# A two-layer transformer block: compressed scores in fp32r halves, later column splits on GpSimd, and one gathered u row per plain expert column

## The reference

```python
kc = compress(k_cmp, cmp_k_w1, cmp_k_w2)                      # 31 compressed keys
s_c = jnp.einsum('bqgrd,bngd->bgrqn', qblk, kc) * scale
p_c = masked_softmax(s_c, cmp_end[None, :] <= t[:, None])
...
mixed = jnp.concatenate([rmsnorm_2(o_a, out_gain_a), rmsnorm_2(o_b, out_gain_b)], axis=-1) @ w_out
h = x + mixed
...
vals, ci = lax.top_k(cand, P_TOPK)                            # 16 picks e, gates g per head
a = jnp.einsum('cd,ckd->ck', xc, expert_u[ec])
w = (gc * jax.nn.gelu(a.astype(jnp.float32))).astype(x.dtype)
y = jnp.einsum('ck,ckd->cd', w, expert_v[ec])
```

## Time and profile before

| what | value |
|---|---|
| device time, 3 runs | median 2398.34 us (2397.9 to 2403.95) |
| the profiled execution | 2400.16 us |
| its span | 2398.3 us |
| mean granted PE clock | 0.998 of full speed |
| busy: PE, DVE, ACT, POOL | 2370.4 (99%), 1706.7 (71%), 822.8 (34%), 1088.0 (45%) us |
| attention | about 967 to 1119 us from the span's start |
| plain u columns, spread, last plain u columns | 1279 to 1553, 1553 to 1801, 1801 to 1868 us |
| v columns | 1875 to 2394 us |

### The profile page before, as it was taken

The page is one execution under the profiler, slowest core; times in us unless marked ns, Lnnn a source line. Parts: engine busy times, 40 slices in busy tenths (PEclk is TensorE's granted clock), DMA queues, the critical chain, the costliest instruction groups (busy, mean ns, idle before and its releaser), DMA issues.

```text
span 2398.3 us, 35569 instructions
## 1 busy us (share of the span) xinstructions
PE 2370.4 (99%) x12528; PEld 2056.0 (86%) x12528; DVE 1706.7 (71%) x2818; ACT 822.8 (34%) x1401; POOL 1088.0 (45%) x711
## 2 busy tenths in 40 slices
PE   8999999999999999999999999999999999999999
PEld 6888888878888887888889999999999888888887
DVE  8888885463433656784718699798886788888887
ACT  4132222100112314675325333344443333333333
POOL 6777766666666550100654888721112322222220
PEclk9999999999999999999999999999999999999999
DMA  4333324333332222200224899999999999999995
GB/s 150 97 105 105 105 86 136 132 109 110 133 119 96 88 81 87 74 4 7 72 95 134 293 311 306 308 350 347 343 332 409 376 361 348 356 355 355 347 361 197
DMA packets 181336, 490.46 MB, mean 205 GB/s; under 512 B 14848, under 2 KB 80512, under 8 KB 181248
## 3 DMA queue, kind: packets, MB, share of 16 engines
q1 hardware_dynamic: 144384, 355.12, 43.5%
q0 software_dynamic: 36864, 134.23, 15.0%
HBM read 436.86 MB, written 52.43 MB: 204 GB/s over the span
## 4 chain that ended last, share of the span: by engine, by line
PE 91%; POOL 3%; issue 3%; DVE 1%; ACT 1%; DMA 0%; SPq 0%; DVEq 0%; POOLq 0%; ACTq 0%
PE ps L726 40%; PE ps L1327 22%; PE ps L1287 18%; POOL spl L2669 2%; PE ps L1161 2%; PE ps L1308 2%; PE ps L1138 1%; POOL rare L2679 1%; PE ps L1124 1%; PE ps L910 1%; PE ps L1084 1%; PE ps L1030 1%; PE ps L831 0%; PE ps L1128 0%; PE ps L1127 0%
## 5 line engine op out<-in xcount | busy, mean ns | idle before, releaser
L1287 PE MATMUL ps<-hh,spl 128*128 128x384 f32 x2048 | 535.3, 337 | 2.9 <-POOL spl L2669 2.9
L726 PE MATMUL ps<-hh,spl 128*128 128x512 f32 x1728 | 535.3, 389 | 1.5 <-DVE x L1978 0.8
L1327 PE MATMUL ps<-spl,wsp 128*128 128x512 f32 x2304 | 523.8, 389 | 0.0
L1327 PEld LDWEIGHTS ps<-spl,wsp 128*128 128x128 f32 x2304 | 432.1, 188 | 89.2
L1691 ACT ACTIVATE spl<-ring 128x1024 fp32r<-128x1024 f32 x256 | 271.9, 1062 | 679.9 <-PE ps L1327 331.9
L2574 POOL TENSOR_TENSOR spl<-ring,spl 128x1024 fp32r<-128x1024 f32 (+1 forms) x164 | 427.7, 2608 | 13.1
L726 PEld LDWEIGHTS ps<-hh,spl 128*128 128x128 f32 x1728 | 324.4, 188 | 69.5 <-DVE x L1978 1.2
L1287 PEld LDWEIGHTS ps<-hh,spl 128*128 128x128 f32 x2048 | 371.1, 188 | 6.0 <-issue 5.4
L2572 POOL CAST spl<-ring 128x1024 fp32r<-128x1024 f32 (+1 forms) x164 | 185.8, 1133 | 400.6 <-PE ps L726 380.1
L1287 PE MATMUL ps<-hl,spl 128*128 128x384 f32 x1024 | 342.5, 334 | 0.0
L2473 DVE TENSOR_TENSOR spl<-ring,spl 128x1024 fp32r<-128x1024 f32 x192 | 235.2, 1225 | 148.5 <-ACT spl L1691 140.4
(11 more groups left out here) (443 smaller groups left out, 3375.1 us busy)
## 6 DMA issues: line engine op xcount, KB each, us to landing
ring<-stream_in SPq DMA_DIRECT2D x134, 512.0 KB
ring<-u_in SPq DMA_DIRECT2D x128, 512.0 KB
ring<-v_in SPq DMA_DIRECT2D x128, 512.0 KB
ring<-stream_in SPq DMA_DIRECT2D x60, 704.0 KB
gelu<-gst SPq DMA_DIRECT2D x128, 192.0 KB
dense<-stage SPq DMA_DIRECT2D x12, 2048.0 KB
gl<-gelu SPq DMA_DIRECT2D x32, 768.0 KB, 7.1
gw<-dense SPq DMA_DIRECT2D x32, 768.0 KB, 9.6
```

The source lines that it names most:

```text
L726: m = pe.matmul(ps[:, bank, :], w[:, part, k0 + k * n:k0 + k * n + P], rhs(k), start=first and k == 0 and part == 0 and rhs is high, stop= ...
L1287: m = pe.matmul(ps[:, bank, 0:TD], w[:, part, k0 + k * P:k0 + (k + 1) * P], rhs(k), start=first and k == 0 and part == 0 and rhs is high, ...
L1327: m = pe.matmul(ps[:, bank, :], wsp[:, j % 2, part, tok], spl[:, j % 2, row, cols], start=False, stop=last and n == 2)
```

## The change

1. `kcz` becomes 2 groups x 2 parts (high, low) x 32 in fp32r, with a zero in the 32nd place. DVE makes it in three dependent steps (one product, four casts, four subtractions) in place of four products; the compressed scores are eight fp32r matmuls in place of four float32 ones; readers of the scores step over 32 columns in place of 31.
2. The bias of a step is a TENSOR_SCALAR with a per-partition scalar in place of a TENSOR_TENSOR.
3. POOL's four output-projection columns of the attention stretch all come in quarters, behind the second, fifth, eighth and last weighing of a branch, in place of: two whole ones behind `mid_ready`, one behind the third weighing, one behind the last.
4. `A_ROOT` is two steps later and stands ahead of the evacuation of its iteration; `A_TURNS` and `A_INVERSE` are two steps later.
5. `gathers_by(e)` is one per column from 12 to 63, 52 in all; `AMONG_DOTS` is 44 (before 50), `EARLY_DOTS` 52 (before 58). The spread keeps 8 a pass, so 28 dots are left beside the last plain columns (before 22).
6. Tiles behind `kcz` move by 128 elements; nothing else is done with them.

```diff
-AMONG_DOTS, EARLY_DOTS, SPREAD_DOTS = 50, 58, 8
+AMONG_DOTS, EARLY_DOTS, SPREAD_DOTS = 44, 52, 8
...
-PLACED, FIRST_DOTS, LAST_DOTS = 12, 16, 60
+PLACED = 12
...
 def gathers_by(e):
 
-    if e < FIRST_DOTS:
-        return min(2 * (e - PLACED + 1), ROW_SLOTS)
-    return ROW_SLOTS + AMONG_DOTS * min(e - FIRST_DOTS + 1, LAST_DOTS - FIRST_DOTS + 1) // (LAST_DOTS - FIRST_DOTS + 1)
+    return e - PLACED + 1
...
-        kcz = sb("kcz", [P, A_G, N_CMP], c=two)
+        kcz = sb("kcz", [P, A_G, 2, P // TT], F32R, c=two)
...
-        A_SQUARES, A_ROOT = A_H * PER + 6, A_H * PER + 10
-        A_TURNS = [A_H * PER + 13 + 4 * k for k in range(TT)]
+        A_SQUARES, A_ROOT = A_H * PER + 6, A_H * PER + 12
+        A_TURNS = [A_H * PER + 15 + 4 * k for k in range(TT)]
...
-        A_INVERSE = A_H * PER + 14
+        A_INVERSE = A_H * PER + 16
...
                     for t in range(TT):
-                        pe.matmul(bank[:, t * N_CMP:(t + 1) * N_CMP], query(at, g)[:, t * P:(t + 1) * P].bitcast(F32), kcz[:, g, :],
-                                  start=t == 0, stop=False)
+                        for part in range(2):
+                            pe.matmul(bank[:, t * CMP_ROWS:(t + 1) * CMP_ROWS], query(at, g)[:, t * P:(t + 1) * P], kcz[:, g, part, :],
+                                      start=t == 0 and part == 0, stop=False)
...
             for u in range(NS + TURN_LAG):
                 if u < NS:
                     probs(*STEPS[u])
+                if u == A_ROOT:
+                    eng.wait_ge(o_squares, TT)
+                    o_inverse_root(NORM_SUMS[0])
                 if u >= TURN_LAG and not on_dve(u - TURN_LAG):
                     turned(u - TURN_LAG)
                 if A_SQUARES <= u < A_SQUARES + TT:
...
-                elif u == A_ROOT:
-                    eng.wait_ge(o_squares, TT)
-                    o_inverse_root(NORM_SUMS[0])
                 elif u - 1 in A_TURNS:
...
-                    o = dve.tensor_tensor(s_[:, 3:4], s_[:, 0:1], root_of(n, qt), ALU.mult)
+                    o = dve.tensor_scalar(s_[:, 3:4], s_[:, 0:1], root_of(n, qt), None, ALU.mult)
...
-            for g in range(A_G):
-                lo, part = slice(g * A_D, (g + 1) * A_D), slice(g * N_CMP, (g + 1) * N_CMP)
-                for half in halves:
-                    o = dve.tensor_tensor(kcz[half, g, :], kcn[lo, 0, part], ps[lo, 6 + (3 + B_H) % 2, part], ALU.mult)
+            step(dve.tensor_tensor(kcn[:, 0, :], kcn[:, 0, :], ps[:, 6 + (3 + B_H) % 2, 0:A_G * N_CMP], ALU.mult))
+            placed = [(g, half, kcn[g * A_D:(g + 1) * A_D, 0, g * N_CMP:(g + 1) * N_CMP]) for g in range(A_G) for half in halves]
+            for g, half, normed in placed:
+                o = dve.tensor_copy(kcz[half, g, 0, 0:N_CMP], normed)
+            step(o)
+            for g, half, normed in placed:
+                o = dve.tensor_tensor(kcz[half, g, 1, 0:N_CMP], normed, kcz[half, g, 0, 0:N_CMP].bitcast(F32), ALU.subtract)
             o.then_inc(mid_ready, 1)
...
                 if c < 4:
-                    if c < 2:
-                        pool.wait_ge(mid_ready, 1)
-                        unit_parts(u % RING, N_SPLIT + c + 1, w=out_w[c])
-                        continue
-                    pool.wait_ge(at_weighed, 3 if c == 2 else A_DONE)
+                    pool.wait_ge(at_weighed, (2, 5, 8, A_DONE)[c])
```

More of the change, by code:

```diff
@@ L309, in build @@
         kz = sb("kz", [P, 2 * A_G, T], F32R, c=two)
-        kcz = sb("kcz", [P, A_G, N_CMP], c=two)
+        kcz = sb("kcz", [P, A_G, 2, P // TT], F32R, c=two)
+        sb("kcz_end", [P, 62], c=two)
         pre = ExitStack()
@@ L342, in build @@
         w7 = sb("w7", [P, 2, D], F32R, c=two)
-        sb("w7_end", [P, 3, T], c=two)
         a_parts = [(oah[:, k, :], oah[:, 4 + k, :] if k < 2 else il1[:, k - 2, :]) for k in range(4)]
@@ L1117, in scores @@
                     for t in range(TT):
-                        pe.matmul(bank[:, t * N_CMP:(t + 1) * N_CMP], query(at, g)[:, t * P:(t + 1) * P].bitcast(F32), kcz[:, g, :],
-                                  start=t == 0, stop=False)
-                    pe.matmul(bank[:, 0:TT * N_CMP], identb[:, :], cmpb[:, :, :].rearrange("p a n -> p (a n)"),
+                        for part in range(2):
+                            pe.matmul(bank[:, t * CMP_ROWS:(t + 1) * CMP_ROWS], query(at, g)[:, t * P:(t + 1) * P], kcz[:, g, part, :],
+                                      start=t == 0 and part == 0, stop=False)
+                    pe.matmul(bank[:, 0:P].rearrange("p (t n) -> p t n", t=TT)[:, :, 0:N_CMP], identb[:, :], cmpb[:, :, :],
                               start=False, stop=True).then_inc(at_s, 1)
@@ L1615, in probs @@
                         o = eng.activation(pr[:, u // TT % 2, u % TT, t * CMP_ROWS:t * CMP_ROWS + N_CMP],
-                                           ps[:, u % TT, t * N_CMP:(t + 1) * N_CMP], ACT.Exp, bias=bias[:, t:t + 1],
+                                           ps[:, u % TT, t * CMP_ROWS:t * CMP_ROWS + N_CMP], ACT.Exp, bias=bias[:, t:t + 1],
                                            scale=root_of(n, t), accum_out=total[:, t:t + 1])
@@ L2237, in tops @@
                     top = cmp_state(n)[0]
-                    step(dve.tensor_reduce(top, ps[:, u % TT, 0:TT * N_CMP].rearrange("p (t n) -> p t n", t=TT), AX_X, ALU.max,
+                    step(dve.tensor_reduce(top, ps[:, u % TT, 0:P].rearrange("p (t n) -> p t n", t=TT)[:, :, 0:N_CMP], AX_X, ALU.max,
                                            negate=True))
@@ L2259, in early_bias @@
                 biases(*STEPS[u])
+            for g in range(A_G):
+                for part in range(2):
+                    dve.tensor_copy(kcz[:, g, part, N_CMP:], zero[:, :])
             for h in range(4):
@@ L2649, in _ @@
                 if c < 4:
-                    if c < 2:
-                        pool.wait_ge(mid_ready, 1)
-                        unit_parts(u % RING, N_SPLIT + c + 1, w=out_w[c])
-                        continue
-                    pool.wait_ge(at_weighed, 3 if c == 2 else A_DONE)
+                    pool.wait_ge(at_weighed, (2, 5, 8, A_DONE)[c])
                     slot, w = u % RING, out_w[c]
-                    pool.tensor_copy(w[:, 0, :], ring[:, slot, 0:D]).then_inc(wt_high, 1)
+                    pool.tensor_copy(w[:, 0, 0:D], ring[:, slot, 0:D]).then_inc(wt_high, 1)
                     pool.wait_ge(wt_high, N_SPLIT + c + 1)
```

## The result

The changed kernel takes 2410.62 us (median of 8 runs, 2407.55 to 2415.81) against 2400.78 (8 runs, 2397.9 to 2403.95); the ratio is 1.0043, with a 95% interval of 1.0034 to 1.0051. It is slower, by about 10 us. The profiled execution took 2410.3 us, its span is 2408.4, the mean granted PE clock 0.996.

The account below looks back on a forecast made before the run. PE, busy 99% of the span, was taken as the bound. Attention start -1.0, compressed scores 0, root and chunks +3.4, one gather per column +3.1 and six gathers +0.5 gave +6.0 us: 2404.3 us, range 2393 to 2412.

Parts of the forecast that it names:

- the likeliest case: Whole kernel: the summed forecast, 2404.3 us for the median; 2398 to 2409 got chance 0.45.
- D: Last plain columns: six more dots and gathers cost +0.5 us, bounds 0 and +7.5.
- A's new places: Attention: POOL's moved output columns could hold only DVE's small products, with PE's scores four steps ahead: 0.
- B: MLA attention: moving the root and the mixing chunks two steps later costs +3.4 us.
- Start of attention: First compressed scores: POOL's hold and its half clock go, later keys bring a 1.9 us wait and half clock: -1.0 us.
- Compressed scores: Attention heads: eight fp32r passes cost the same as four float32 matmuls' eight passes: 0, bounds +-0.8 us in all.
- Root and chunks: MLA attention: root's wait and clock gain, four 1.4 us waits for ACT and one half clock cost: +3.4 us.
- One gather per column: Plain u columns: 5.3 us gained, but a 7 us wait for the picks' read and half clock: +3.1 us net.
- Six more gathers beside the last plain columns: Last plain u columns: full DMA engines take 3.1 MB more, DVE holds: +0.5 us, bounds 0 and +7.5.
- Rival 3: Last plain columns: six gathers' 7.5 us all return as late ring loads, +7 more, 2411 us; chance 0.12.
- Rival 2: MLA stretch: each of four 1.4 us waits is followed by half clock, 2409.4 us; chance 0.25.
- rival 1: Attention and gathers: chunk turns don't wait, start keeps full clock, gather 51 lands soon: -9 us, 2389; chance 0.12.

Follow-up runs that it names:

- e5: Changed kernel with POOL's first three output columns behind the third, sixth and ninth weighing instead of second, fifth and eighth: 2408.05 us (one run).
- e7: Changed kernel with the compressed keys in plain float32 again, with scores, readers and DVE's making as before the change: 2409.05 us (one run).
- e4: Changed kernel with the mixing chunks and the inverse back at their old places, the root left two steps later: 2406.36 us, ratio 1.0023.
- e2: Changed kernel with its 52 gathers out by column 60, double at columns 12, 13 and 14: 2406.24 us, ratio 1.0017.
- e3: Changed kernel without the transfers of the last six gathers of u rows, their dots kept: 2404.39 us, ratio 1.0012.
- g3: g1 with 55 gathers by column 60, three columns double, 25 left for the last plain columns: 2392.5 us, ratio 0.996.
- g4: g2 with the three early 1.5 MB loads behind ring loads of columns 125, 126, 127 instead of 123, 125, 127: 2396.36 us, ratio 0.9979.
- g1: Changed kernel with float32 keys, POOL's columns behind weighings 3, 6, 9, chunks back, 58 gathers by column 60 from column 9: 2389.64 us, ratio 0.9953.
- g2: g1 with 52 gathers, one per column from 9 to 60, 28 left for the last plain columns: 2394.6 us, ratio 0.9974.

## Why the prediction was right, and where not

The forecast was 2404.3 us within 2393 to 2412, with 0.50 on no difference that can be told and 0.38 on slower. The measured 2410.6 is in the range and on the side that had 0.38: the likeliest case was 6 us short. (By the shares given to the rivals, slower adds up to 0.25 + 0.12 + 0.045 = 0.415.) That it stayed in the range is in part luck, since an error in one term made up for others: D was 7.2 too low and A's new places 1.6, B was 2.5 too high, and the start of attention 0.3. With B as forecast it would have come to about 2413.

- **Start of attention** (-1.0): PE's waits ahead of and behind the first compressed scores and the half clock sum to -1.3 (+1.1, then -2.4). The wait for the keys was given as 1.9 and is 2.06, the one of 1.94 behind it is gone, and half clock followed. Right.
- **"In their new places only DVE's small products could be held ... 0"**: wrong. Three heads grew from 11.2 to 11.73 to 11.75 us, +1.6 in all: the held product stands ahead of a turn's evacuation on DVE, and the turn that PE starts behind it comes 0.5 us later, of which 0.31 shows as a wait. e5 shows that the place of POOL's column decides it. The third column before the change stood behind a window's weighing (the third), where it cost nothing: from the second head on all were at 11.2. What failed here is that scores four steps ahead were taken to cover any such hold; PE also waits for evacuations, and they are not four steps ahead.
- **Compressed scores** (0): right, 1.04 us for eight fp32r passes against 1.05, and heads of the same length in e7. The floor of the Trainium skill (page "TensorE: Matmul & The Clock Gate", section "Back-to-back issue gap", about 25 ns for 1 to 64 columns) does not set this pace here: a pass takes 0.13 us.
- **Root and chunks** (+3.4): the mechanism is right, waits of 1.08 three times and 1.42 for ACT where 1.4 was given, and the root's wait is 0.55. Two sizes were off. Three of the waits are 0.3 shorter, since the handing over that I put at 0.25 us is nearly nothing: ACT's three operations take 1.7 us from first start to last end, and begin as PE's chunk ends. And none was followed by half clock. The term is +0.9; e4 gives +3.6 for the chunks and -2.7 for the root.
- **One gather per column** (+3.1): +3.3. The wait was given as 7 and is 6.70, the landing 6.2 and is 5.98, the 5.3 us gained are in the trace (unit 61 starts 5.1 us earlier counted from column 12), and half clock follows. e2 shows the cause by undoing it alone.
- **Six more gathers beside the last plain columns** (+0.5): this is the step that failed. "I take +0.5, near the bound of no wait". It measured +7.7, at the other bound (5.15 us of waiting and half clock behind it). The argument was that PE did not wait there. That says nothing on how near the ring loads were to late. e3 shows the cause by leaving out the transfers alone (7.5 us less). That the bound of 7.5 fits so well is luck in part: it priced the transfers alone, while the measured term is a wait of 5.15 and 2.5 of half clock; and three gathers, 3.7 us of the engines, cost 1.5 us in g3. Rival 3, which had 0.12, is what happened, together with a cheaper part B.

Rival 2 (four drops in the MLA stretch) did not happen; rival 1 would have needed a landing within 3 us. With D at its upper bound the sum would have been 2411.3.

## What to carry to other kernels

A stretch in which the DMA engines are full and PE never waits has no reserve to show: an added transfer there can cost its whole time and the half clock behind the wait (three gathers of 3.7 us cost 1.5 here, six of 7.5 us cost 7.7 to 8.0). Look at how long loads take to land, not only at whether anyone waits. When work is spread evenly over a loop, its last piece moves to the loop's end; ask what is read right behind it. And move one thing at a time in a hand-written order: the root's two steps were worth 2.7 us and the chunks' two steps cost 3.6.

## What had not been expected of the hardware

- A product of two SBUF tiles on DVE, 128 x 4 and normally 0.16 us, is held to 0.77 beside POOL's copy of 128 x 1024, and a 128 x 1 product to 0.49 beside a quarter of 128 x 256. The hold lasts as long as POOL's instruction, so what counts is how much of that is left: before the change a 128 x 4 product took 1.83 beside a whole 128 x 1024 low half. The same bias as a TENSOR_SCALAR takes 0.20 to 0.22 in these places. The Trainium skill (page "SBUF — State Buffer", section "Who interferes with whom") says that a DVE instruction with two SBUF inputs contends with a GpSimd instruction that reads SBUF; the trace agrees (0.77 against 0.16). It also has TENSOR_SCALAR among the operations that can be held when they run in a two-port mode; on these 128 x 1 operands it was not (0.20).
- Half clock behind a wait is partly chance. From 1500 us on, there was a stretch of it behind every wait of 4 us and more; behind the one of 8.1 us at the very start of the kernel there was none (windows of 1.00). The wait of 2.0 to 2.07 us ahead of the first compressed scores was followed by it in all seven profiles that had it, but not for equally long: windows of 4 us at 0.60 and 0.97 in one execution and at 0.86, 0.50 and 0.78 in another. As an estimate, 4 us times what these lack to 1, that is a loss of 1.7 us in the one and 3.4 in the other. The same wait at 1.03 us (float32 keys) was followed by it in two profiles, those of g3 and g4, and not in three, e7, g1 and g2; from the first to the second compressed scores it took 9.72 to 9.75 us without it and 11.33 and 12.45 with it. The waits of 1.08 and 1.42 in the MLA stretch were never followed by it, in seven profiles with four such waits each.
- A ring load of half a megabyte took up to 20.75 us in the full stretch, while the median gather of as many bytes landed in 9.2.
